# Second expert layer: GpSimd takes every second row addition of the gathered tokens

## The chip, the cores and the metric

The kernel runs on one core of one Trainium2 chip. The time is device microseconds of one execution; a comparison takes the median of several. The profile is of one execution, and its times count from the first instruction.

## The reference, cut to what matters

The program is one decoder layer. A normalised input goes through a gated delta mixer and a sparse attention mixer, then through an expert layer, and is normalised at the end. Only the second half of the expert layer matters here. There are 16384 experts, and each is one row of `expert_u` and one row of `expert_v`, both of 1024 numbers. Each of the 512 tokens picks 16 experts for each of 8 heads, so 128 in all.

```python
    def block(xb):
        ...
        eidx = jnp.take_along_axis(cidx, pos, axis=-1)
        gates = jax.nn.softmax(top_s, axis=-1)
        u = expert_u[eidx]
        vv = expert_v[eidx]
        act = jax.nn.gelu(jnp.einsum('nhkd,nd->nhk', u, xb).astype(F32), approximate=False)
        return jnp.einsum('nhk,nhkd->nd', (gates * act).astype(vv.dtype), vv)
```

The last line is the stage that is changed: for each token, the sum of its 128 rows of `expert_v`, each times its gate and its activation.

## The kernel before

The stages follow each other: input projection, delta mixer, sparse attention, output projection, routing with the first expert table (`route_stage`, to about 1453 us), the second expert table (`value_stage`, from about 1455 to 2007 us), final norm (`final_stage`). In each stage every engine has a program of its own, in the order in which it is written, and semaphores tie them together.

`value_stage` treats the tokens in two ways.

The first 384 tokens (`TD`) take the whole table. The table comes in 128 tiles `v_raw` of 128x1024. A tile's turn, number `e`, goes so:

- SyncE loads `v_raw` (L1522) and the activations `act_s` (L1525) for turn `e` four turns ahead, and once in eight turns a block of gates.
- VectorE forms `w`, activation times gate, 128x384 (L1566).
- ScalarE makes `v_hi`, the table tile rounded for the fast matmul (L1537), and `w_hi` from `w` (L1539).
- VectorE makes the remainders `v_lo` (128x1024) and `w_lo` (128x384), both at L1554.
- TensorE adds 24 matmuls to eight banks: for each of 8 slices the products high by high, high by low, low by high (L1589 to L1591). It waits for `v_low` and `w_low` of its turn. At the end it raises `second`, which frees the two buffers `v_hi` and `v_lo` of that parity. ScalarE waits for it before the `v_hi` of two turns on.

The last 128 tokens, one in each partition, take only their own rows. GpSimd gathers with an indirect DMA (L1547) row `k` of every token into one of four places of `ring`. VectorE adds it into `own`, times the column `k` of the weights `w_own` (L1574). In the trace `ring` is `va_ring`, `own` is `va_own`, `w_own` is `own_weights`. One gathered row belongs to each turn, and VectorE adds it at the end of the turn. GpSimd issues the gather of row `k` as soon as VectorE has added row `k - 4` (semaphore `added`). When all is done, TensorE transposes `own` into the banks (L1603), and the next stage adds the banks to the residual.

So VectorE's order in each turn is `w`, `v_lo`, `w_lo`, `own`. The order is written by hand.

## Time and profile before

| | us |
|---|---|
| median of 3 runs | 2022.57 |
| lowest and highest | 2022.33, 2024.21 |
| the profiled execution's own time | 2029.51 |
| its span, first to last instruction | 2027.7 |
| busy in the span: TensorE | 1777.1 |
| busy: VectorE | 1474.5 |
| busy: ScalarE | 699.0 |
| busy: GpSimd | 471.3 |

The profiled execution takes 7 us longer than the median run, of which the span leaves out 1.8 us. The three runs lie within 1.9 us of each other, 0.1%.

Busy time over the whole span mixes stages. The last quarter of the span is `value_stage` alone, and it is read by itself. A matmul's busy time is modelled, so the pace of TensorE is read from how far apart the starts of repeating operations lie, not from the mean of one. VectorE's operations overlap by some hundredths of a microsecond, so their cost in a row is also read from start to start.

### The profile page before, as it was taken

Reading aid. Unit: us, or ns where it says so; the run is one execution under the profiler, and the core shown is the slowest. Engines: PE = TensorE matmul, PEld = TensorE weight load, DVE = VectorE, ACT = ScalarE, POOL = GpSimd, SP = SyncE. Lnnn points to the kernel's source line nnn. Section 1 sums busy time; section 2 is a strip of 40 time slices with the busy share of each in tenths; the row PEclk is TensorE's granted clock in tenths of the full one; section 3 lists DMA queues with packets and bytes.
Section 4 is the critical chain, followed back from the end, with each engine's and each line's share of the span. In section 5 each row is a group of like instructions: output and inputs, shape, how many; then the busy total and the mean of one; then the engine's idle time right before and its main releaser. Section 6 shows DMA issues by size and latency. Waiting matters only on the chain. (4 is left out here: it accounts for less than half of the span.)

```text
span 2027.7 us, 29145 instructions
## 1 busy us (share of the span) xinstructions
PE 1777.1 (88%) x9881; PEld 1595.0 (79%) x9881; DVE 1474.5 (73%) x2561; ACT 699.0 (34%) x1053; POOL 471.3 (23%) x324
## 2 busy tenths in 40 slices
PE   6995789798779889669799999777599999999997
PEld 4874776434558789669699999777599999999996
DVE  4787542399532399898999999666577888887886
ACT  4652121434332233223344444222133333333333
POOL 1000000000110155444233333455422222222220
PEclk9998886758899889789899999899899999999999
DMA  3320000100213345334398888999899999999993
GB/s 107 103 81 21 1 1 0 54 0 1 73 54 102 107 140 179 92 113 142 122 327 330 320 304 335 332 329 332 286 329 355 336 362 330 363 330 361 332 363 124
DMA packets 148988, 404.23 MB, mean 199 GB/s; under 512 B 14228, under 2 KB 71700, under 8 KB 145464
## 3 DMA queue, kind: packets, MB, share of 16 engines
q1 hardware_dynamic: 108600, 243.97, 35.8%
q0 software_dynamic: 36864, 134.23, 17.8%
q10 hardware_dynamic: 3456, 25.17, 3.0%
q8 instruction: 36, 0.59, 0.1%
q14 instruction: 32, 0.26, 0.0%
HBM read 350.88 MB, written 52.44 MB: 199 GB/s over the span
## 5 line engine op out<-in xcount | busy, mean ns | idle before, releaser
L1458 PE MATMUL bank<-h_hi,rt_u_hi 128*128 128x384 f32 x1024 | 365.9, 357 | 85.4 <-POOL rt_u_lo L1267 44.0
L1589 PE MATMUL bank<-va_w_hi,va_v_hi 128*128 128x384 f32 x1024 | 343.3, 335 | 19.8 <-DVE va_w_lo L1554 19.8
L1459 PE MATMUL bank<-h_lo,rt_u_hi 128*128 128x384 f32 x1024 | 355.0, 347 | 0.0
L1460 PE MATMUL bank<-h_hi,rt_u_lo 128*128 128x384 f32 x1024 | 354.5, 346 | 0.0
L1590 PE MATMUL bank<-va_w_lo,va_v_hi 128*128 128x384 f32 x1024 | 343.2, 335 | 0.0
L1591 PE MATMUL bank<-va_w_hi,va_v_lo 128*128 128x384 f32 x1024 | 343.0, 335 | 0.0
L1221 ACT ACTIVATE rt_u_hi<-rt_u_raw 128x1024 fp32r<-128x1024 f32 x128 | 135.5, 1058 | 414.5 <-PE bank L1460 403.0
L1458 PEld LDWEIGHTS bank<-h_hi,rt_u_hi 128*128 128x128 f32 x1024 | 202.6, 198 | 94.6 <-POOL rt_u_lo L1267 42.8
L1537 ACT ACTIVATE va_v_hi<-va_v_raw 128x1024 fp32r<-128x1024 f32 x128 | 135.7, 1060 | 357.3 <-PE bank L1591 341.1
L1273 POOL DMA_INDIRECT h<-u_rows_dram,own_experts x128 | 188.6, 1474 | 285.7 <-DVE rt_waste L1367 278.2
L1554 DVE TENSOR_TENSOR va_v_lo<-va_v_raw,va_v_hi 128x1024 fp32r<-128x1024 f32 x128 | 156.8, 1225 | 103.7 <-ACT va_v_hi L1537 98.9
L1547 POOL DMA_INDIRECT va_ring<-v_dram,own_experts x128 | 129.9, 1015 | 412.3 <-DVE va_own L1574 396.5
L1589 PEld LDWEIGHTS bank<-va_w_hi,va_v_hi 128*128 128x128 f32 x1024 | 193.1, 189 | 20.0 <-DVE va_v_lo L1554 20.0
L1459 PEld LDWEIGHTS bank<-h_lo,rt_u_hi 128*128 128x128 f32 x1024 | 202.5, 198 | 0.0
L1460 PEld LDWEIGHTS bank<-h_hi,rt_u_lo 128*128 128x128 f32 x1024 | 201.8, 197 | 0.0
L1367 DVE SCALAR_TENSOR_TENSOR rt_waste<-h,rt_h_tok 128x1024 bf16<-128x1024 f32 x128 | 156.4, 1222 | 61.8 <-DMA h<-u_rows_dram,own_experts 59.0
L1590 PEld LDWEIGHTS bank<-va_w_lo,va_v_hi 128*128 128x128 f32 x1024 | 193.1, 189 | 0.0
L1591 PEld LDWEIGHTS bank<-va_w_hi,va_v_lo 128*128 128x128 f32 x1024 | 193.1, 189 | 0.0
L1267 POOL TENSOR_TENSOR rt_u_lo<-rt_u_raw,rt_u_hi 128x1024 fp32r<-128x1024 f32 x48 | 130.6, 2725 | 237.2 <-ACT rt_u_hi L1221 237.1
L1574 DVE SCALAR_TENSOR_TENSOR va_own<-va_ring,own_weights,va_own 128x1024 f32<-128x1024 f32 x128 | 163.6, 1278 | 0.0
L1360 DVE TENSOR_TENSOR rt_u_lo<-rt_u_raw,rt_u_hi 128x1024 fp32r<-128x1024 f32 x80 | 97.8, 1223 | 3.9 <-ACT rt_u_hi L1221 2.4
L878 POOL TENSOR_SCALAR_AFFINE_SELECT dsa_score<-dsa_score 128x128 f32<-128x128 f32 x3 | 0.9, 314 | 424.0 <-DVE dsa_score L911 424.0
(316 smaller groups left out, 2909.9 us busy)
## 6 DMA issues: line engine op xcount, KB each, us to landing
rt_u_raw<-u_dram SPq DMA_DIRECT2D x128, 512.0 KB
va_v_raw<-v_dram SPq DMA_DIRECT2D x128, 512.0 KB
active_scratch<-rt_act SPq DMA_DIRECT2D x128, 192.0 KB
gates_scratch<-rt_early ACTq DMA_DIRECT2D x24, 1024.0 KB
va_gate<-gates_scratch SPq DMA_DIRECT2D x16, 1536.0 KB
va_act<-active_scratch SPq DMA_DIRECT2D x128, 192.0 KB
in_raw<-w_in_dram SPq DMA_DIRECT2D x22, 512.0 KB, 3.3
query_raw<-w_query_dram SPq DMA_DIRECT2D x16, 512.0 KB, 3.3
```

The costliest lines, as they stand in the source:

```text
L1221: a(u_hi[:, j % 2, :], u_raw[:, j % 4, :], ACT.Copy).then_inc(u_high, 1)
L1273: nc.gpsimd.indirect_dma_start(out=ring[:, k % RING, :], out_offset=None, in_=u_rows, in_offset=bass.IndirectOffsetOnAxis(ap=eidx[:, k:k + ...
L1367: d.scalar_tensor_tensor(waste[:], ring[:, r, :], 1.0, h_tok[:], ALU.mult, ALU.mult, accum_out=dots[:, bass.ds(k, 1)]).then_inc(s["dot"], 1)
L1458: mm(bank, u_hi[:, j % 2, cols], hi[:, c, 0:TD], start=c == 0, stop=False)
L1459: mm(bank, u_hi[:, j % 2, cols], lo[:, c, 0:TD], start=False, stop=False)
L1460: last = mm(bank, u_lo[:, j % 2, cols], hi[:, c, 0:TD], start=False, stop=c == DC - 1)
L1537: nc.scalar.activation(v_hi[:, par, :], v_raw[:, j, :], ACT.Copy).then_inc(v_high, 1)
L1554: nc.vector.tensor_tensor(out, a, high.bitcast(F32), ALU.subtract).then_inc(done, 1)
L1574: nc.vector.scalar_tensor_tensor(own[:], ring[:, j, :], w_own[:, bass.ds(e, 1)], own[:], ALU.mult, ALU.add).then_inc(added, 1)
L1589: mm(bank, v_hi[:, j, cols], w_hi[:, j, :], start=start, stop=False)
L1590: mm(bank, v_hi[:, j, cols], w_lo[:, j, :], start=False, stop=False)
L1591: last = mm(bank, v_lo[:, j, cols], w_hi[:, j, :], start=False, stop=stop)
```

## The change

The gathered rows are split by parity. Rows with even `k` are added by VectorE as before. Rows with odd `k` are added by GpSimd, in two operations: a multiply of the row by its weight column into `term` (a `tensor_scalar`), and an addition of `term` to an accumulator of GpSimd's own, `own_odd`. GpSimd waits for its own multiply by the semaphore `weighed`, and for its own last addition by `added_odd`. It issues the gather of row `k + 4` behind row `k`: for an even row after VectorE has added it, for an odd one behind its own addition. At the end VectorE adds `own_odd` to `own` once, and TensorE waits for that. Two tiles of 4 KB a partition are new.

```diff
@@ value_stage @@
+        ring, own, own_odd, term = sb("ring", [P, RING, D]), sb("own", [P, D]), sb("own_odd", [P, D]), sb("term", [P, D])
...
             @block.gpsimd
             def _(pool):
-                for k in range(N):
-                    if k >= RING:
-                        pool.wait_ge(added, k - RING + 1)
+                def gather(k):
                     nc.gpsimd.indirect_dma_start(
                         out=ring[:, k % RING, :], out_offset=None, in_=v_rows,
                         in_offset=bass.IndirectOffsetOnAxis(ap=eidx[:, k:k + 1], axis=0)).then_inc(rows_in[k % RING], 16)
+
+                for k in range(RING):
+                    gather(k)
+                nc.gpsimd.memset(own_odd[:], 0.0).then_inc(added_odd, 1)
+                for k in range(N):
+                    if k % 2:
+                        pool.wait_ge(rows_in[k % RING], 16 * (k // RING + 1))
+                        pool.wait_ge(added_odd, k // 2 + 1)
+                        nc.gpsimd.tensor_scalar(term[:], ring[:, k % RING, :], w_own[:, k:k + 1], None,
+                                                ALU.mult).then_inc(weighed, 1)
+                        pool.wait_ge(weighed, k // 2 + 1)
+                        nc.gpsimd.tensor_tensor(own_odd[:], own_odd[:], term[:], ALU.add).then_inc(added_odd, 1)
+                    else:
+                        pool.wait_ge(added, k // 2 + 1)
+                    if k + RING < N:
+                        gather(k + RING)
...
                         minus(w_lo[:, par, :], w[:, par, :], w_hi[:, par, :], w_low)
+                        if k % 2:
+                            continue
                         dve.wait_ge(rows_in[j], 16 * turn)
                         if not (head and k == 0):
-                            dve.wait_ge(added, e)
+                            dve.wait_ge(added, 4 * u + k // 2)
                         nc.vector.scalar_tensor_tensor(own[:], ring[:, j, :], w_own[:, bass.ds(e, 1)], own[:],
                                                        ALU.mult, ALU.add).then_inc(added, 1)
...
                 run(dve, eight)
+                dve.wait_ge(added, N // 2)
+                dve.wait_ge(added_odd, N // 2 + 1)
+                nc.vector.tensor_tensor(own[:], own[:], own_odd[:], ALU.add).then_inc(added, 1)
...
-                pe.wait_ge(added, N)
+                pe.wait_ge(added, N // 2 + 1)
```

VectorE at the start of the stage before the change: the clearing of `va_own`, then the first turn and three operations of the second.

```order
L1576 MEMSET va_own 128x1024
L1566 TENSOR_TENSOR va_w<-va_act,va_gate 128x384
L1554 TENSOR_TENSOR va_v_lo<-va_v_raw,va_v_hi 128x1024
L1554 TENSOR_TENSOR va_w_lo<-va_w,va_w_hi 128x384
L1574 SCALAR_TENSOR_TENSOR va_own<-va_ring,own_weights,va_own 128x1024
L1566 TENSOR_TENSOR va_w<-va_act,va_gate 128x384
L1554 TENSOR_TENSOR va_v_lo<-va_v_raw,va_v_hi 128x1024
L1554 TENSOR_TENSOR va_w_lo<-va_w,va_w_hi 128x384
```

The same place after the change, with the first pair of turns and the first operation of the next.

```order
L1592 MEMSET va_own 128x1024
L1580 TENSOR_TENSOR va_w<-va_act,va_gate 128x384
L1568 TENSOR_TENSOR va_v_lo<-va_v_raw,va_v_hi 128x1024
L1568 TENSOR_TENSOR va_w_lo<-va_w,va_w_hi 128x384
L1590 SCALAR_TENSOR_TENSOR va_own<-va_ring,own_weights,va_own 128x1024
L1580 TENSOR_TENSOR va_w<-va_act,va_gate 128x384
L1568 TENSOR_TENSOR va_v_lo<-va_v_raw,va_v_hi 128x1024
L1568 TENSOR_TENSOR va_w_lo<-va_w,va_w_hi 128x384
L1580 TENSOR_TENSOR va_w<-va_act,va_gate 128x384
```

The operation on `va_own` stands only in every second turn, and in the others `w` of the next turn follows `w_lo` at once.

GpSimd at the start of the stage, as one piece of the difference. Before, its program there is nothing but 128 gathers.

```order
 L1143 UNCONDITIONAL_BRANCH
 L1542 UNCONDITIONAL_BRANCH
-L1547 DMA va_ring<-v_dram,own_experts 128x1024 x128
+L1545 DMA va_ring<-v_dram,own_experts 128x1024 x4
+L1551 MEMSET va_own_odd 128x1024
+L1545 DMA va_ring<-v_dram,own_experts 128x1024
+L1556 TENSOR_SCALAR va_term<-va_ring,own_weights 128x1024
+L1559 TENSOR_TENSOR va_own_odd<-va_own_odd,va_term 128x1024
+L1545 DMA va_ring<-v_dram,own_experts 128x1024 x2
+L1556 TENSOR_SCALAR va_term<-va_ring,own_weights 128x1024
```

Now the gathers stand two by two between pairs of operations: of the two, the first is that of the odd row behind GpSimd's addition, the second that of the even row, which waits for VectorE.

## Rows read from the trace of the kernel before

**Rows 1.** Three stretches: busy time (operations) by engine, granted clock, DMA share, GB/s.

```profile
1370.00:1380.00 10.00, 7.81 (x44) 7.17 (x42) 7.22 (x12) 1.63 (x3) 4.74 (x4) 1.00 0.98 341
1500.00:1600.00 100.00, 100.00 (x579) 100.00 (x578) 80.76 (x97) 35.49 (x49) 24.47 (x25) 1.00 0.96 345
1900.00:2000.00 100.00, 100.00 (x579) 100.00 (x578) 80.60 (x96) 35.49 (x49) 22.11 (x22) 1.00 0.88 312
```

**Rows 2.** Groups of 1500 to 2000 us: busy us, mean ns | idle before, and releaser.

```profile
L1589 PE MATMUL bank<-va_w_hi,va_v_hi 128*128 128x384 f32 x962 | 321.3, 334 | 0.0
...
L1554 DVE TENSOR_TENSOR va_v_lo<-va_v_raw,va_v_hi 128x1024 fp32r<-128x1024 f32 x120 | 147.0, 1225 | 96.2 <-ACT va_v_hi L1537 91.4 <-issue 4.8
L1537 ACT ACTIVATE va_v_hi<-va_v_raw 128x1024 fp32r<-128x1024 f32 x121 | 128.3, 1060 | 325.2 <-PE bank L1591 325.2
...
L1554 DVE TENSOR_TENSOR va_w_lo<-va_w,va_w_hi 128x384 fp32r<-128x384 f32 x120 | 66.2, 551 | 0.0
```

**Rows 3.** Timeline of VectorE, one turn: start us, length us, operation.

```profile
1704.75 1.23 DVE L1554 TENSOR_TENSOR va_v_lo<-va_v_raw,va_v_hi 128x1024 fp32r<-128x1024 f32 x1 [0.74 <-ACT va_v_hi L1537]
1705.89 0.55 DVE L1554 TENSOR_TENSOR va_w_lo<-va_w,va_w_hi 128x384 fp32r<-128x384 f32 x1
1706.36 1.28 DVE L1574 SCALAR_TENSOR_TENSOR va_own<-va_ring,own_weights,va_own 128x1024 f32<-128x1024 f32 x1
1707.56 0.55 DVE L1566 TENSOR_TENSOR va_w<-va_act,va_gate 128x384 f32<-128x384 f32 x1
```

**Rows 4.** Timeline at the stage's end: VectorE's last `own`, TensorE's transposes.

```profile
2001.78 1.28 DVE L1574 SCALAR_TENSOR_TENSOR va_own<-va_ring,own_weights,va_own 128x1024 f32<-128x1024 f32 x1
...
2007.14 1.04 PE L1603 MATMUL bank<-cst,va_own 128*128 128x128 f32 x8
```

**Rows 5.** Timeline of the same turn: ScalarE's `v_hi` and GpSimd's gather.

```profile
1707.88 1.06 ACT L1537 ACTIVATE va_v_hi<-va_v_raw 128x1024 fp32r<-128x1024 f32 x1 [2.75 <-PE bank L1591]
...
1707.92 1.01 POOL L1547 DMA_INDIRECT va_ring<-v_dram,own_experts  x1 [3.09 <-DVE va_own L1574]
```

**Rows 6.** Timeline, GpSimd and VectorE with two-input operations at the same time.

```profile
782.73 2.39 POOL L1267 TENSOR_TENSOR rt_u_lo<-rt_u_raw,rt_u_hi 128x1024 fp32r<-128x1024 f32 x1 [2.22 <-ACT rt_u_hi L1221]
782.96 2.44 DVE L1316 TENSOR_TENSOR rt_cand<-rt_val 128x256 f32<-128x256 f32 x1
...
967.59 2.29 DVE L1336 TENSOR_TENSOR rt_early<-rt_part_f,cst 128x2048 f32<-128x2048 f32 x1
968.11 3.97 POOL L1267 TENSOR_TENSOR rt_u_lo<-rt_u_raw,rt_u_hi 128x1024 fp32r<-128x1024 f32 x1 [10.31 <-ACT rt_u_hi L1221]
969.91 4.33 DVE L1338 TENSOR_TENSOR rt_early<-rt_early,rt_num_f 128x2048 f32<-128x2048 f32 x1
972.04 4.44 POOL L1267 TENSOR_TENSOR rt_u_lo<-rt_u_raw,rt_u_hi 128x1024 fp32r<-128x1024 f32 x1
```

**Rows 7.** GpSimd's one-input select by its line: duration ns min/median/max, shape.

```profile
L878 POOL TENSOR_SCALAR_AFFINE_SELECT dsa_score<-dsa_score x3: 294/294/353, 406.3 to 459.9; 128x128 f32<-128x128 f32 x3
...
L882 POOL TENSOR_SCALAR_AFFINE_SELECT dsa_bias<-dsa_bias x1: 1917/1917/1917, 461.5 to 461.5; 128x2048 f32<-128x2048 f32 x1
```

**Rows 8.** Timeline of `route_stage`: gathers beside VectorE's two-input operations.

```profile
1366.33 0.94 POOL L1273 DMA_INDIRECT h<-u_rows_dram,own_experts  x1 [1.27 <-DVE rt_waste L1367]
1366.44 1.22 DVE L1367 SCALAR_TENSOR_TENSOR rt_waste<-h,rt_h_tok 128x1024 bf16<-128x1024 f32 x1 [0.38 <-DMA h<-u_rows_dram,own_experts]
1367.59 1.22 DVE L1360 TENSOR_TENSOR rt_u_lo<-rt_u_raw,rt_u_hi 128x1024 fp32r<-128x1024 f32 x1
1367.95 1.68 POOL L1273 DMA_INDIRECT h<-u_rows_dram,own_experts  x1 [0.68 <-DVE rt_waste L1367]
```

5 lines of the change are left out of this document (2 added, 3 removed).

## The prediction, made before the change was run

> **What bounds the kernel now.** I read the table by stretches first. From 1500 us to the end of the second expert layer TensorE is busy all the time at a granted clock of 1.00, while VectorE is busy 81% and GpSimd 24% [rows 1]. The groups of that stretch say the same from the other side. TensorE's matmuls have 0.0 us of idle time ahead of them, and ScalarE's split of the table tile waits 325.2 us for "PE bank", which is the release of its buffer by the matmuls [rows 2]. So TensorE sets the end, and VectorE waits for ScalarE, which waits for TensorE: 91.4 us ahead of its `v_lo` [rows 2].
>
> Next the order of time within one tile, a tile being one of the 128 turns with 24 matmuls. The starts of `own` at 1706.36 and at 2001.78 lie 71 tiles apart, so a tile takes 295.42 / 71 = 4.16 us and a pair of tiles 8.32 us [rows 3, 4]. In it VectorE issues four operations. From start to start `v_lo` takes 1.14 us, `w_lo` 0.47 and `own` 1.20; `w`, of the same shape as `w_lo`, I put at 0.47. That is 3.28 us of work and 0.88 us of waiting [rows 3]. Its lead over TensorE is small: `w_lo` ends at 1706.44, and the tile before, whose end releases ScalarE's `v_hi`, ends just ahead of 1707.88 [rows 3, 5]. So `w_lo` is ready some 1.3 us before TensorE wants it. That lead, and not the 19% of idle time, is what may be spent.
>
> **What the change takes off VectorE.** One `own` in each pair: 64 times 1.20 us. TensorE does not wait for `own` in the loop, so this alone is worth nothing. VectorE's work in a pair falls from 6.56 to 5.36 us.
>
> **What it puts on GpSimd.** In each pair a multiply (one tensor input and a column) and an addition (two inputs), both 128x1024. Neither stands in this stretch now. The nearest row for the addition is GpSimd's subtraction of the same size, 2.39 us when nothing is in its way [rows 6]. For the multiply it is the one-input affine select: 0.294 us for 128 columns and 1.917 us for 2048, so 0.845 ns a column and 1.05 us for 1024 [rows 7].
>
> GpSimd by itself keeps up. A pair costs two gather issues, 1.01 us [rows 5], or 1.68 us where one meets a VectorE operation [rows 8], besides 1.05 and 2.39. That is 1.01 + 1.68 + 1.05 + 2.39 = 6.1 us of 8.32, with 2 us left for the gaps between them.
>
> **The two engines exclude each other.** This is the row on which everything turns. At 782.73 GpSimd begins its 2.39 us; VectorE's addition of two inputs, issued at 782.96, takes 2.44 us and ends 0.28 us behind GpSimd's end [rows 6]. At 967.59 VectorE begins a two-input operation of 2.29 us; GpSimd's, issued at 968.11, takes 3.97 us in place of 2.39. VectorE's next takes 4.33 and GpSimd's next 4.44: they take turns, whole instruction by whole instruction [rows 6]. All four VectorE operations of a tile read two tiles from SBUF. So the time of both engines adds up, and I take it as one queue.
>
> Prices in that queue. GpSimd's two-input operation ends 972.08 - 969.88 = 2.20 us after VectorE's end, the next 976.48 - 974.24 = 2.24 [rows 6]: 2.22 us for the addition, 0.17 less than alone, since its start is hidden. The multiply, with the same 0.17 hidden, holds the queue 0.88 us; with nothing hidden 1.05. A VectorE operation behind a GpSimd turn costs a little less than its start-to-start time: the one of 2.29 us ended 974.24 - 972.08 = 2.16 us after it, where about 2.21 would follow from the 0.08 us overlap of `v_lo` and `w_lo` [rows 3, 6]. Twice 0.05 us comes off. The sum for a pair:
>
> 5.36 + 2.22 + 0.88 - 0.10 = 8.36 us at least, 8.53 us with the multiply unhidden.
>
> Against TensorE's 8.32 us that is 0.04 to 0.21 us too much, and I take the middle, 8.44 us, since the multiply is issued right where VectorE is about to begin `w_lo` and may get ahead of it with its start unhidden. TensorE then waits for `w_lo` 0.12 us in each of 64 pairs, 7.7 us, less the 1.3 us of lead used up first: 6.4 us.
>
> The bounds. No row has a one-input GpSimd operation beside a two-input VectorE operation. If it holds nothing up, the queue has 7.48 us in a pair and TensorE stays the bound: 0 us. If the multiply costs what the two-input form does, a pair has 5.36 + 2.22 + 2.20 - 0.10 = 9.68 us: 1.36 x 64 - 1.3 = 86 us. I stay at one input, because the row with one input is near in kind and its cost is proportional to the columns [rows 7].
>
> The Trainium skill (SBUF — State Buffer, "Who interferes with whom") says that a VectorE instruction with two SBUF inputs contends with a GpSimd instruction that reads SBUF, with whoever issues first holding the shared pair for the whole instruction. The trace agrees for two inputs on both sides, as 4.33 us for an operation of 2.29 us shows. By its wording the multiply counts too, which gives the 8.36 to 8.53 us above; a rule by which only two-input GpSimd operations counted would give the 7.48 us and no loss.
>
> **The other edits.** The gathers: now each is issued 0.28 us behind the end of `own` [rows 3, 5]. The even ones stay there; the odd ones are queued behind multiply and addition, and so come 4 to 6 us later in the pair. A gather first waits for a running VectorE operation (1.68 us at 1367.95 in place of 0.94) but does not hold up the next one (1.22 us at 1366.44) [rows 8]. It is 4 rows, or 16.6 us, ahead of use, so later by 6 us it still lands in time; the DMA engines, at 96% busy and 345 GB/s [rows 1], are asked for no more bytes. Cost 0, covered by the ring. GpSimd's waiting for `added` holds up only gathers behind it, with the same cover. The `memset` of the second accumulator lies in the time before the first table tile is there: 0. VectorE's last addition of the two accumulators costs 1.2 us. It follows GpSimd's last addition, which ends 0.47 + 1.14 + 0.88 + 0.47 + 2.22 = 5.2 us behind the last `own` (`w`, `v_lo`, multiply, `w_lo`, addition), and so is over at about 6.5 us. TensorE now ends 2007.14 - 2003.06 = 4.1 us behind the `own` of the last tile [rows 4], and the last `own` will be that of the tile before, so 4.1 us further from the end, less the lead that is used up: about 7 us. Cost 0, with about 1 us of cover; without cover at most 1.2 us.
>
> TensorE's clock: 0.12 us of waiting in 8.4 should not lower it. At 1370 to 1380 us TensorE was busy 7.81 us of 10 and was still granted 1.00 [rows 1].
>
> **The forecast.** The profiled execution took 2029.51 us, the median of the runs is 2022.57 us. The change adds 6.4 us: 2035.9 us for a profiled execution, 2029.0 us for the median, 0.3% slower.
>
> **Rivals.**
> 1. No difference. The multiply does not exclude VectorE, or holds the queue less than 0.85 us. Then a pair is at most 8.38 us and the loss under 4 us: 2022.6 to 2026 us. For it: the sum misses TensorE's 8.32 us by 0.04 us at its lower end. Against it: every two-input row shows full exclusion, and what VectorE is denied is its second reader's turn, whatever GpSimd does with what it reads. This is the rival on the other side; it decides at 0.9 us of held time.
> 2. The multiply is dear, a rate above 0.845 ns a column. Each 0.1 us of it costs 6.4 us: at one and a half times the price +0.5 us, 2061 us, at the two-input price 2109 us. Against it: the one-input row. For it: that row is another operation, and it reads no scalar column.
> 3. The feed becomes the bound: odd gathers, or table tiles that are issued behind a later `v_lo`, land late at 96% DMA load [rows 1]. ScalarE never waited for a table tile in 121 turns [rows 2], and a wait of 1 us every eighth tile would be 16 us: 2045 us.
> 4. Faster. VectorE freed of `own` could only help if TensorE waited for it, and its idle time ahead of the matmuls is 0.0 us [rows 2].
>
> **How the numbers follow.** The bound of what can be told from no change is 0.2%, or 4 us. Forecast, a pair between 8.38 and 8.6 us: 50%. Rival 1: 35%. Rival 2 from 20 us upwards: 8%. Rival 3: 4%. Rival 4: 3%. Slower is the forecast and rivals 2 and 3: 0.62; same 0.35; faster 0.03. The range runs from 2021 us, which takes in rival 1 with some scatter, to 2048 us, which takes in the sum with a multiply 0.2 us dearer and rival 3; outside lie most of rival 2 and all of rival 4 that counts.
>
> **What would show it.** In the changed profile VectorE's `v_lo`, `w_lo` or `w` must show means above 1.225 and 0.551 us, by some 3 us in a pair in all, and GpSimd's addition more than 2.39 us. The multiply's shortest time should be near 1.05 us. The starts of `own` should lie 8.44 us apart, and TensorE's first matmul of a tile should have waits for `w_lo` of about 0.1 to 0.2 us. If `w_lo` and `v_lo` keep their lengths beside the multiply, rival 1 is right; if the multiply takes over 1.3 us, rival 2; if ScalarE waits for the table tile, rival 3. The forecast fails altogether if the exclusion does not add up as one queue, for example when one engine is held up without the other gaining.

## The result, and the profile after

The changed kernel takes 2107.39 us (median of 4 runs, 2105.73 to 2109.73) against 2023.39 us for the kernel before (median of 4). The ratio is 1.041, with a 95% interval of 1.039 to 1.043. So it is slower, as forecast, but by 84 us and not by 6. The time lies 59 us above the top of the forecast range. The profiled execution took 2105.73 us, its span 2103.5 us.

The first view is the groups of the changed kernel between 1500 and 2000 us. Its columns are those of [rows 2]: line, engine, operation, tiles, shapes, count, then busy time and mean ns of one, then idle time ahead and its releaser.

```profile
L1608 PE MATMUL bank<-va_w_hi,va_v_hi 128*128 128x384 f32 x832 | 282.2, 339 | 54.3 <-DVE va_w_lo L1568 54.3
...
L1556 POOL TENSOR_SCALAR va_term<-va_ring,own_weights 128x1024 f32<-128x1024 f32 x53 | 179.4, 3384 | 2.2
L1568 DVE TENSOR_TENSOR va_w_lo<-va_w,va_w_hi 128x384 fp32r<-128x384 f32 x104 | 170.9, 1643 | 0.0
L1559 POOL TENSOR_TENSOR va_own_odd<-va_own_odd,va_term 128x1024 f32<-128x1024 f32 x52 | 167.2, 3215 | 4.3
...
L1568 DVE TENSOR_TENSOR va_v_lo<-va_v_raw,va_v_hi 128x1024 fp32r<-128x1024 f32 x104 | 126.7, 1218 | 60.3 <-ACT va_v_hi L1537 60.3
```

TensorE, which had 0.0 us of idle time ahead of its matmuls [rows 2], now waits for `w_lo`. `w_lo` has grown from 551 ns to a mean of 1643, while `v_lo` kept its length. GpSimd's multiply takes 3384 ns. The waits of the same stretch (who waits for whom, us in all, times, longest) give the count:

```profile
ACT va_v_hi L1537 <- PE bank L1610: 266.3, 104, 2.8
...
PEld bank L1608 <- issue: 69.3, 52, 1.3
DVE va_v_lo L1568 <- ACT va_v_hi L1537: 60.3, 52, 1.2
PE bank L1608 <- DVE va_w_lo L1568: 54.3, 52, 1.1
POOL va_ring L1545 <- DVE va_own L1590: 30.0, 52, 0.6
```

TensorE's weight load stands still 69.3 / 52 = 1.33 us in every pair of tiles, and 64 pairs of that are 85 us. So the whole loss is TensorE standing still once in each pair. And VectorE is not the engine that is always at work: it still waits 60.3 / 52 = 1.16 us in every pair for `v_hi`, and `v_hi` waits for TensorE. Both wait, for each other.

Busy time by engine (PE, PEld, DVE, ACT, POOL), granted clock, DMA share and GB/s in a stretch of the stage, to be held against [rows 1]:

```profile
1700.00:1800.00 100.00, 89.54 (x504) 86.64 (x503) 87.81 (x74) 31.61 (x42) 91.33 (x42) 1.00 0.90 298
```

TensorE's clock stayed at 1.00, its level of 2.4 GHz, although TensorE is busy 89.5% and no more all the time. DMA fell from 345 to 298 GB/s with the pace, and nobody waits for it. GpSimd is busy 91%, and waits for `own` only 30.0 / 52 = 0.58 us in a pair.

Now one pair in order of time (start, duration, engine, operation, idle time ahead). VectorE of the changed kernel, first the `w_lo` of the pair before:

```profile
1705.50 2.74 DVE L1568 TENSOR_TENSOR va_w_lo<-va_w,va_w_hi 128x384 fp32r<-128x384 f32 x1
1708.16 1.27 DVE L1590 SCALAR_TENSOR_TENSOR va_own<-va_ring,own_weights,va_own 128x1024 f32<-128x1024 f32 x1
1709.36 0.55 DVE L1580 TENSOR_TENSOR va_w<-va_act,va_gate 128x384 f32<-128x384 f32 x1
1709.83 1.21 DVE L1568 TENSOR_TENSOR va_v_lo<-va_v_raw,va_v_hi 128x1024 fp32r<-128x1024 f32 x1
1710.96 0.55 DVE L1568 TENSOR_TENSOR va_w_lo<-va_w,va_w_hi 128x384 fp32r<-128x384 f32 x1
1711.43 1.39 DVE L1580 TENSOR_TENSOR va_w<-va_act,va_gate 128x384 f32<-128x384 f32 x1
1714.00 1.22 DVE L1568 TENSOR_TENSOR va_v_lo<-va_v_raw,va_v_hi 128x1024 fp32r<-128x1024 f32 x1 [1.19 <-ACT va_v_hi L1537]
1715.14 2.74 DVE L1568 TENSOR_TENSOR va_w_lo<-va_w,va_w_hi 128x384 fp32r<-128x384 f32 x1
1717.81 1.27 DVE L1590 SCALAR_TENSOR_TENSOR va_own<-va_ring,own_weights,va_own 128x1024 f32<-128x1024 f32 x1
```

GpSimd and ScalarE at the same time:

```profile
1709.70 1.01 POOL L1545 DMA_INDIRECT va_ring<-v_dram,own_experts  x1 [0.57 <-DVE va_own L1590]
1710.76 3.39 POOL L1556 TENSOR_SCALAR va_term<-va_ring,own_weights 128x1024 f32<-128x1024 f32 x1
1714.23 3.24 POOL L1559 TENSOR_TENSOR va_own_odd<-va_own_odd,va_term 128x1024 f32<-128x1024 f32 x1
```

```profile
1712.91 1.06 ACT L1537 ACTIVATE va_v_hi<-va_v_raw 128x1024 fp32r<-128x1024 f32 x1 [2.45 <-PE bank L1610]
```

The starts of `own` lie 1717.81 - 1708.16 = 9.65 us apart, where [rows 3, 4] give 8.32. The 9.65 us are a closed loop: a tile's turn on TensorE frees the buffers that the same side (even or odd) needs for its tile two turns on, and TensorE can't begin that tile before its `w_lo`. The even side can be walked:

- 1708.24: the `w_lo` before this pair ends (1705.50 + 2.74). TensorE begins the even tile, which takes 4.16 us.
- 1712.91: the buffer it frees lets `v_hi` start, 0.51 us after 1708.24 + 4.16. `v_hi` takes 1.06 us.
- 1714.00: `v_lo`, then `w_lo`, which would end 0.47 us behind `v_lo` but is held by the addition issued at 1714.23. The addition is held itself until `v_lo` ends at 1715.22. From there to its end at 1717.47 are 2.25 us, close to the 2.20 and 2.24 us of [rows 6].
- 1717.88: `w_lo` ends, and TensorE begins. 1717.88 - 1708.24 = 9.64 us.

Without the hold of 2.19 us (2.74 less 0.55) the loop takes 7.45 us. It has 0.87 us to spare against TensorE's 8.32, so the hold costs 2.19 - 0.87 = 1.32 us in each pair. This is no test yet, because the 0.87 us are worked out from the same pair. The kernel before gives nearly the same: there `w_lo` ends at 1706.44 and, if the same 0.51 us lie ahead of `v_hi`, the tile at 1707.88 - 0.51 = 1707.37, 0.93 us later [rows 3, 5]. Whether 0.87 us also holds for other holds and places is what the experiments show. Nothing of VectorE's 1.16 us of idle time helps, because it lies in front of the `v_lo` of this very loop. That is the theory which the experiments test: call it LOOP. The rival, QUEUE, is the prediction's own sum with a dearer multiply. A third, GPSIMD BOUND, says that GpSimd's own chain of gather, multiply, addition and gather fills the pair.

### The profile page after: what moved, and what is told of

Same layout as the page of the kernel before. It is cut to its first block and busy times, and to the rows that moved or that the text cites. A ratio compares the mean times of both kernels' runs of the same rounds, so it can differ in the third digit from the quotient of the medians.

```text
span 2103.5 us, 29156 instructions
## 1 busy us (share of the span) xinstructions
PE 1792.2 (85%) x9881; PEld 1591.9 (76%) x9881; DVE 1582.6 (75%) x2498; ACT 706.1 (34%) x1053; POOL 900.7 (43%) x453
## 5 line engine op out<-in xcount | busy, mean ns | idle before, releaser
L1608 PE MATMUL bank<-va_w_hi,va_v_hi 128*128 128x384 f32 x1024 | 348.5, 340 | 83.0 <-DVE va_w_lo L1568 83.0
L1556 POOL TENSOR_SCALAR va_term<-va_ring,own_weights 128x1024 f32<-128x1024 f32 x64 | 217.6, 3400 | 5.8 <-DVE va_own L1590 3.3
L1559 POOL TENSOR_TENSOR va_own_odd<-va_own_odd,va_term 128x1024 f32<-128x1024 f32 x64 | 202.5, 3165 | 5.3
L1568 DVE TENSOR_TENSOR va_w_lo<-va_w,va_w_hi 128x384 fp32r<-128x384 f32 x128 | 203.2, 1588 | 0.0
```

Source lines behind the costliest of these rows:

```text
L1556: nc.gpsimd.tensor_scalar(term[:], ring[:, k % RING, :], w_own[:, k:k + 1], None, ALU.mult).then_inc(weighed, 1)
L1559: nc.gpsimd.tensor_tensor(own_odd[:], own_odd[:], term[:], ALU.add).then_inc(added_odd, 1)
L1568: nc.vector.tensor_tensor(out, a, high.bitcast(F32), ALU.subtract).then_inc(done, 1)
L1608: mm(bank, v_hi[:, j, cols], w_hi[:, j, :], start=start, stop=False)
```

## The experiments

The loss or gain of each is against runs of the kernel before on the same chip; its medians there were 2022.6 to 2025.5 us. Where an edit is shown, lines with - are those of the changed kernel.

### What the GpSimd operations cost and hold

A block behind the end of the program runs each GpSimd operation alone, twice in a row, and then once beside a row of VectorE additions of two inputs, 128x1024.

```diff
+                ops = [
+                    lambda: g.tensor_scalar(term[:], row, col, None, ALU.mult),
...
+                    lambda: g.affine_select(out=term[:], in_=row, pattern=[[1, D]], base=0, channel_multiplier=1,
+                                            compare_op=ALU.is_ge, fill=0.0),
...
+                    lambda: g.tensor_tensor(term[:], row, ring[:, 1, :], ALU.add),
+                ]
```

> The changed kernel, with a block of extra operations between the second expert layer and the final norm; nothing else is changed. In the block GpSimd first works alone: each of seven operations twice (multiply by a column 128x1024, 128x512 and 128x128, multiply by a constant, the select, a copy, a two-input addition). Then VectorE issues 24 two-input additions of 128x1024 back to back beside six of GpSimd's. Three theories of the 84 us. LOOP: the multiply is long (2.8 us alone) but holds VectorE up for only 0.9 us of it; the addition then falls between v_lo and w_lo of the even tile, on the path ScalarE split, v_lo, w_lo, TensorE, which two buffers close into a loop. QUEUE: the multiply holds VectorE up for 2.2 us like a two-input operation, and the pair is the plain sum of both engines' held times. GPSIMD BOUND: GpSimd's own chain of gather, multiply, addition, gather fills the pair. Expected here: LOOP and GPSIMD BOUND: column multiply alone 2.7 to 2.9 us, about 2.6 ns a column; beside VectorE one VectorE operation grows by 0.8 to 1.1 us. QUEUE: the same operation grows by 2.2 us or more. All: addition alone 2.39 us, and one VectorE operation grows by 2.2 us beside it. The total is 30 to 70 us above the changed kernel and says nothing.

The program took 2162.49 us with the added block. GpSimd's timeline alone (x2: two in a row, the duration is of both):

```profile
2080.42 5.78 POOL L1640 TENSOR_SCALAR va_term<-va_ring,own_weights 128x1024 f32<-128x1024 f32 x2 [2.78 <-ACTq L1627]
2086.30 3.22 POOL L1641 TENSOR_SCALAR va_term<-va_ring,own_weights 128x512 f32<-128x512 f32 x2
2089.61 1.30 POOL L1642 TENSOR_SCALAR va_term<-va_ring,own_weights 128x128 f32<-128x128 f32 x2
...
2096.71 2.15 POOL L1644 TENSOR_SCALAR_AFFINE_SELECT va_term<-va_ring 128x1024 f32<-128x1024 f32 x2
```

The multiply takes 2.9 us (5.78 / 2) and the affine select of the same size 1.07. A plain copy takes 1.07 as well, a multiply by a constant 2.8. So the price in the forecast, 1.05 us, was that of the wrong operation. But what a VectorE operation of 1.21 us grows to beside the multiply, and then beside the two-input addition, is:

```profile
2108.21 2.06 DVE L1662 TENSOR_TENSOR va_v_raw<-va_v_raw 128x1024 f32<-128x1024 f32 x1
```

```profile
2118.39 3.35 DVE L1662 TENSOR_TENSOR va_v_raw<-va_v_raw 128x1024 f32<-128x1024 f32 x1
```

The multiply holds VectorE 0.85 us once, in spite of its 2.9 us. The addition holds it 2.14 us. Copy, select and both multiplies hold it alike. The held times of the forecast, 0.88 and 2.22 us, were therefore right.

### The same instructions in another order, and each half alone

First the same instructions, with each addition issued one pair later, behind the next `own`:

```diff
-                        nc.gpsimd.tensor_tensor(own_odd[:], own_odd[:], term[:], ALU.add).then_inc(added_odd, 1)
                     else:
                         pool.wait_ge(added, k // 2 + 1)
+                        if k:
+                            add(k // 2 - 1)
```

> The same instructions as the changed kernel on every engine; only GpSimd's order differs: the addition of an odd row is issued after VectorE's next own, ahead of the gather of the even row, and not right behind its multiply. LOOP: the addition now runs beside w and v_lo of the odd tile with TensorE's lead of about 1.3 us over it, and the multiply beside the even tile, so a pair falls from 9.65 us to 8.4 to 8.8 us: 2025 to 2050 us. QUEUE: the sum of held times is the same, 9.6 us a pair: 2100 to 2110 us. GPSIMD BOUND: the same work on GpSimd, so again about 9.3 to 9.7 us a pair: 2085 to 2110 us.

It took 2081.67 us (ratio 1.030, 1.026 to 1.033), 26 us less than the changed kernel. That is above the range of LOOP and just below those of QUEUE and GPSIMD BOUND, so each theory missed. GpSimd's timeline in it:

```profile
1799.19 1.60 POOL L1545 DMA_INDIRECT va_ring<-v_dram,own_experts  x1 [0.27 <-POOL va_term L1560]
1800.83 2.41 POOL L1554 TENSOR_TENSOR va_own_odd<-va_own_odd,va_term 128x1024 f32<-128x1024 f32 x1
1803.40 1.76 POOL L1545 DMA_INDIRECT va_ring<-v_dram,own_experts  x1 [0.16 <-POOL va_own_odd L1554]
1805.19 2.88 POOL L1560 TENSOR_SCALAR va_term<-va_ring,own_weights 128x1024 f32<-128x1024 f32 x1
1808.35 1.60 POOL L1545 DMA_INDIRECT va_ring<-v_dram,own_experts  x1 [0.27 <-POOL va_term L1560]
```

Here GpSimd never waits for VectorE. Its own chain is 1808.35 - 1799.19 = 9.16 us long, with gathers of 1.60 and 1.76 us that met VectorE operations, and it sets the pace. (The loop gives nearly the same here: one `v_lo` in each pair takes 2.95 us, held 1.74, and 8.32 + 1.74 - 0.87 = 9.19 us. That GpSimd waits for nobody is what speaks for its chain.) The chain is a second bound, which the forecast had put at 6.1 us and gaps. GPSIMD BOUND is right for this kernel in its mechanism, though not in its range.

Then the multiply without the addition (the odd rows are missing from the sum), and the addition without the multiply (the odd rows are added without their weights):

```diff
                                                 ALU.mult).then_inc(weighed, 1)
                         pool.wait_ge(weighed, k // 2 + 1)
-                        nc.gpsimd.tensor_tensor(own_odd[:], own_odd[:], term[:], ALU.add).then_inc(added_odd, 1)
```

> The changed kernel without GpSimd's additions: the weighed odd rows are left out of the sum, so the output lacks them. LOOP: the multiply holds 0.9 us once a pair, inside TensorE's lead: 8.32 us a pair, 2023 us, as before the change. QUEUE: 5.26 + 2.2 = 7.5 us of held time, below TensorE's 8.32: also 2023 us. GPSIMD BOUND: 2023 us. What it tells: that it is the addition, where it stands, and not the multiply by itself, that costs; over 2030 us would speak against LOOP.

2031.25 us, ratio 1.004 (1.002 to 1.006). `v_lo` of 2.10 to 2.22 us shows the hold of 0.9 to 1.0 us, most of which the 0.87 us to spare takes up. It still costs 8 us. The expectation had said that over 2030 us would speak against LOOP, so this run does, by 1 us, and the rest of the 8 us is not explained.

```diff
-                        nc.gpsimd.tensor_scalar(term[:], ring[:, k % RING, :], w_own[:, k:k + 1], None,
-                                                ALU.mult).then_inc(weighed, 1)
-                        pool.wait_ge(weighed, k // 2 + 1)
-                        nc.gpsimd.tensor_tensor(own_odd[:], own_odd[:], term[:], ALU.add).then_inc(added_odd, 1)
+                        nc.gpsimd.tensor_tensor(own_odd[:], own_odd[:], ring[:, k % RING, :], ALU.add).then_inc(added_odd, 1)
```

> The changed kernel without GpSimd's multiplies: the odd rows are added without their weights. LOOP: the addition comes 3.4 us earlier in the pair, between v_lo and w_lo of the odd tile, which has 1.3 us of lead for 2.2 us of hold at first; the wait moves own back, and the phases settle at 0 to 0.3 us a pair: 2023 to 2042 us. QUEUE: 5.26 + 2.22 = 7.5 us: 2023 us. GPSIMD BOUND: 2023 us. Above 2060 us would mean that the addition costs wherever it stands.

2066.57 us, ratio 1.022 (1.019 to 1.025), above what any of the theories said. In this kernel GpSimd is idle 3.2 to 4.2 us in a pair, and VectorE has 5.36 + 2.2 = 7.6 us of work. Neither is full; 44 us are lost all the same. A sum of held times cannot give this. The loop can, if every pair is read and not one. VectorE's `v_lo` of the side beside the addition is held in turns by 2.09 and 1.14 us (over its 1.21), and the starts of `own` lie 9.5 and 8.5 us apart in turns, all through 1500 to 2000 us:

```profile
1809.43 3.30 DVE L1566 TENSOR_TENSOR va_v_lo<-va_v_raw,va_v_hi 128x1024 fp32r<-128x1024 f32 x1 [1.01 <-ACT va_v_hi L1537]
...
1818.93 2.35 DVE L1566 TENSOR_TENSOR va_v_lo<-va_v_raw,va_v_hi 128x1024 fp32r<-128x1024 f32 x1 [1.98 <-ACT va_v_hi L1537]
```

Less 0.87 us each, that is 1.22 and 0.27 us in two pairs, 32 times: 48 us, near the 44.

The same addition alone, but issued right behind `own`, ahead of both gathers:

```diff
+                for k in range(0, N, 2):
+                    pool.wait_ge(added, k // 2 + 1)
...
+                    nc.gpsimd.tensor_tensor(own_odd[:], own_odd[:], ring[:, (k + 1) % RING, :], ALU.add).then_inc(added_odd, 1)
                     if k + RING < N:
                         gather(k + RING)
+                        pool.wait_ge(added_odd, k // 2 + 2)
+                        gather(k + 1 + RING)
```

> As the run with the addition only (odd rows added without their weights, 2067 us), but GpSimd issues the addition at once behind VectorE's own, before the two gathers and not between them, some 1.0 us earlier. Same instructions on each engine. LOOP: the addition then runs beside w of the odd tile and the 0.9 us in which VectorE waits anyway, so it delays v_lo by only 1.4 us, against a lead of about 1.3: 8.32 to 8.5 us a pair, 2023 to 2035 us. A theory in which each two-input turn of GpSimd costs the same wherever it is: 2067 us.

2040.08 us, ratio 1.008 (1.006 to 1.010), 5 us above the range of LOOP. The instructions are those of the run before, and moving the addition by one gather is worth 27 us. Here too the holds take turns:

```profile
1804.58 2.55 DVE L1565 TENSOR_TENSOR va_v_lo<-va_v_raw,va_v_hi 128x1024 fp32r<-128x1024 f32 x1 [0.80 <-ACT va_v_hi L1537]
...
1813.33 2.04 DVE L1565 TENSOR_TENSOR va_v_lo<-va_v_raw,va_v_hi 128x1024 fp32r<-128x1024 f32 x1 [1.29 <-ACT va_v_hi L1537]
```

One is of 1.34 us, 0.47 more than the slack, the other of 0.83 us and inside it: 0.47 x 32 = 15 us, and 15 were measured.

### The forecast's own prices: the short operation first

If only the length of the multiply was wrong, a kernel with an operation of 1.05 us in its place, which copies the odd row and leaves out its weight, should land on the forecast.

```diff
-                        nc.gpsimd.tensor_scalar(term[:], ring[:, k % RING, :], w_own[:, k:k + 1], None,
-                                                ALU.mult).then_inc(weighed, 1)
+                        nc.gpsimd.affine_select(out=term[:], in_=ring[:, k % RING, :], pattern=[[1, D]], base=0,
+                                                channel_multiplier=1, compare_op=ALU.is_ge,
+                                                fill=0.0).then_inc(weighed, 1)
```

> The changed kernel with the select in place of the multiply: it copies the row, without the weight, so odd rows are added unweighted; it holds VectorE for the same 0.84 us but is over in 1.07 us in place of 2.88. This is the price that the prediction took. LOOP: the addition is issued about 1.8 us earlier than in the changed kernel, behind the odd tile's v_lo, which has some lead; as with the addition alone (8.8 us a pair) part of it is spent: 8.5 to 9.0 us, 2035 to 2068 us. If the prediction's sum was right but for the multiply's length: 8.44 us, 2029 us. If only held time counted: same as the changed kernel, 2107 us.

2112.6 us, ratio 1.047 (1.040 to 1.055): with the forecast's own prices the loss is 88 us. This is the run that condemns the sum. Its timelines, GpSimd and then VectorE:

```profile
1804.46 2.40 POOL L1560 TENSOR_TENSOR va_own_odd<-va_own_odd,va_term 128x1024 f32<-128x1024 f32 x1
```

```profile
1804.53 3.42 DVE L1569 TENSOR_TENSOR va_v_lo<-va_v_raw,va_v_hi 128x1024 fp32r<-128x1024 f32 x1 [2.03 <-ACT va_v_hi L1537]
...
1814.18 3.42 DVE L1569 TENSOR_TENSOR va_v_lo<-va_v_raw,va_v_hi 128x1024 fp32r<-128x1024 f32 x1 [2.03 <-ACT va_v_hi L1537]
```

The addition is issued 0.07 us ahead of `v_lo` and holds it 2.21 us. By the slack that is (2.21 - 0.87) x 64 = 86 us. A pair takes 9.65 us again, as in the changed kernel, since the hold lies in the same loop, one operation earlier. VectorE is idle 2.03 us and GpSimd 3.18 us in the pair. The expectation of LOOP, 2035 to 2068 us, was missed too: the theory had the mechanism but placed the addition wrongly. The place repeats itself because the addition is issued behind `own`, and `own` moves with the loop.

### The loop opened: four buffers

If the two buffers close the loop, four places each for `v_hi`, `v_lo`, `w`, `w_hi` and `w_lo` open it.

```diff
-        v_hi, v_lo = sb("v_hi", [P, 2, D], F32R), sb("v_lo", [P, 2, D], F32R)
+        v_hi, v_lo = sb("v_hi", [P, 4, D], F32R), sb("v_lo", [P, 4, D], F32R)
...
-                        if not (head and k < 2):
-                            act.wait_ge(second, e - 1)
+                        if not (head and k < 4):
+                            act.wait_ge(second, e - 3)
```

> The changed kernel with four places instead of two for v_hi, v_lo, w, w_hi and w_lo, so that VectorE and ScalarE may be up to three tiles ahead of TensorE; the work and GpSimd's order are the same. LOOP: the loop TensorE, split, v_lo, addition, w_lo, TensorE no longer closes over one tile, so the pair falls from 9.65 us to the larger of the held times (5.26 + 2.2 + 0.84 = 8.3 us) and GpSimd's own chain (1.0 + 2.9 + 2.4 + 1.0 to 1.8 and gaps, 7.7 us and what it waits for VectorE): 8.4 to 9.2 us, 2028 to 2080 us. GPSIMD BOUND: GpSimd is as loaded as before, so the time stays at 2090 to 2107 us. QUEUE is already ruled out by the late addition (2082 us with the same held times).

2062.28 us, ratio 1.018 (1.017 to 1.020): 45 us of the 84 are gone, with all of the change's instructions there. What is left has another cause. GpSimd's additions in it:

```profile
1798.51 3.13 POOL L1559 TENSOR_TENSOR va_own_odd<-va_own_odd,va_term 128x1024 f32<-128x1024 f32 x1
...
1807.46 3.12 POOL L1559 TENSOR_TENSOR va_own_odd<-va_own_odd,va_term 128x1024 f32<-128x1024 f32 x1
```

They lie 8.95 us apart, and between them GpSimd waits for nobody (busy 93.6%, the rest are gaps between its own instructions). VectorE is nearly as full, 97%, because `own` is held here as well, 1.4 us. But it does wait for GpSimd, for rows that are gathered late, 12.0 us in all and 10 times between 1500 and 2000 us, while GpSimd never waits for VectorE. So GpSimd's chain with the long multiply is taken as the bound: (8.95 - 8.32) x 64 = 40 us, and 38 were measured. How much of the chain is VectorE's doing, which holds GpSimd's addition 0.7 us, this run does not separate.

Now the four buffers with the short operation, in which both GpSimd's chain and the loop are out of the way:

```diff
-        v_hi, v_lo = sb("v_hi", [P, 2, D], F32R), sb("v_lo", [P, 2, D], F32R)
+        v_hi, v_lo = sb("v_hi", [P, 4, D], F32R), sb("v_lo", [P, 4, D], F32R)
...
-                        nc.gpsimd.tensor_scalar(term[:], ring[:, k % RING, :], w_own[:, k:k + 1], None,
-                                                ALU.mult).then_inc(weighed, 1)
+                        nc.gpsimd.affine_select(out=term[:], in_=ring[:, k % RING, :], pattern=[[1, D]], base=0,
+                                                channel_multiplier=1, compare_op=ALU.is_ge,
+                                                fill=0.0).then_inc(weighed, 1)
```

> Four places for v_hi, v_lo and the rest, and the select in place of the multiply (odd rows without weights). With two places this first operation gave 2113 us. GpSimd's chain is now short (1.05 + 2.4 and two gathers), and VectorE is decoupled from TensorE, so the prediction's sum should hold: 5.36 + 2.2 + 0.84 - 0.1 = 8.3 us against TensorE's 8.32: 2023 to 2032 us. If the exclusion cost something beyond the sum: 2050 us or more.

2030.33 us, ratio 1.003 (1.000 to 1.005). VectorE's timeline:

```profile
1804.00 1.27 DVE L1591 SCALAR_TENSOR_TENSOR va_own<-va_ring,own_weights,va_own 128x1024 f32<-128x1024 f32 x1
...
1806.80 1.39 DVE L1569 TENSOR_TENSOR va_w_lo<-va_w,va_w_hi 128x384 fp32r<-128x384 f32 x1
1808.12 2.74 DVE L1581 TENSOR_TENSOR va_w<-va_act,va_gate 128x384 f32<-128x384 f32 x1
...
1812.39 1.27 DVE L1591 SCALAR_TENSOR_TENSOR va_own<-va_ring,own_weights,va_own 128x1024 f32<-128x1024 f32 x1
```

A pair takes 8.39 us, with VectorE never idle, one hold of 0.84 and one of 2.19 us. That is the forecast's sum of 8.36 to 8.53 us. The loss of 7 us (1 to 10 by the interval) goes with the forecast's 6.4, but is too small to tell more. The same work in two buffers takes 2112.6. So the sum was right for a kernel whose loop is open, and this kernel's is not.

The control, the kernel before with four buffers (its diff is against the kernel before):

```diff
-        act_s, w = sb("act", [P, 4, TD]), sb("w", [P, 2, TD])
-        w_hi, w_lo = sb("w_hi", [P, 2, TD], F32R), sb("w_lo", [P, 2, TD], F32R)
+        act_s, w = sb("act", [P, 4, TD]), sb("w", [P, 4, TD])
+        w_hi, w_lo = sb("w_hi", [P, 4, TD], F32R), sb("w_lo", [P, 4, TD], F32R)
```

> The control: the kernel before with four places in place of two. TensorE is the bound, so nothing changes: 2021 to 2027 us.

2026.24 us, ratio 1.002 (1.000 to 1.003). More buffers give nothing by themselves; the 3 us more are hardly clear of the noise, and leave 4 us between this kernel and the one ahead of it.

Together the runs make a table of two by two, in us above the kernel before:

| | multiply, 2.9 us | select, 1.07 us |
|---|---|---|
| two buffers | 84 | 88 |
| four buffers | 38 | 7 |

Either the closed loop or GpSimd's long chain is enough to break the forecast. Both have to go before it holds.

### The same time on GpSimd without its reads

In place of multiply and addition, GpSimd writes `term` with memsets, and the odd rows are missing from the sum. Six of them first:

```diff
+                def fill(n):
+                    for _ in range(n):
+                        nc.gpsimd.memset(term[:], 0.0).then_inc(weighed, 1)
...
-                        nc.gpsimd.tensor_scalar(term[:], ring[:, k % RING, :], w_own[:, k:k + 1], None,
-                                                ALU.mult).then_inc(weighed, 1)
-                        pool.wait_ge(weighed, k // 2 + 1)
-                        nc.gpsimd.tensor_tensor(own_odd[:], own_odd[:], term[:], ALU.add).then_inc(added_odd, 1)
+                        fill(6)
```

> The changed kernel with six clearings of a 128x1024 tile (0.96 us each, writes alone) in the place of the multiply and the addition; the odd rows are left out of the sum. GpSimd is as busy as in the changed kernel (some 5.8 us and two gathers in a pair), and its chain behind own is as long. LOOP: what costs is the hold on VectorE's two-input operations between the split and w_lo; if a write alone does not hold them, 2023 to 2027 us. GPSIMD BOUND (its occupancy or its late gathers cost): 2060 us and more. If writes hold VectorE too, v_lo and w_lo will be long in the trace.

2064.02 us, ratio 1.020 (1.016 to 1.023). No VectorE operation was held (`v_lo` 1.225 us), yet the time rose: six memsets take 6.04 us and make with waits and gathers too long a chain, so that rows came late. VectorE's `own` waited 62.2 us in all for them, 23 times. So a chain that is too long costs without any hold, which is what GPSIMD BOUND had said. Five memsets, 5.03 us, are near the 2.88 + 2.39 us of the two operations alone, and fit into the pair:

```diff
-                        fill(6)
+                        fill(5)
```

> The changed kernel with five clearings (5.0 us) in the place of multiply and addition, which take 2.88 + 2.39 = 5.27 us when nothing is in their way; the odd rows are left out of the sum. Six clearings gave 2064 us, with GpSimd never waiting and rows landing late. LOOP: writes hold nothing and five fit: GpSimd's chain is about 0.3 + 1.0 + 5.0 + 0.3 + 1.0 = 7.6 us of 8.32, so 2023 to 2030 us. GPSIMD BOUND: 2050 us and more.

2022.16 us, ratio 1.000 (0.997 to 1.002). Its groups between 1500 and 2000 us:

```profile
L1556 POOL MEMSET va_term<- 128x1024 f32 x300 | 287.7, 959 | 16.4 <-issue 2.6
...
L1572 DVE TENSOR_TENSOR va_v_lo<-va_v_raw,va_v_hi 128x1024 fp32r<-128x1024 f32 x119 | 145.8, 1225 | 165.2 <-ACT va_v_hi L1537 165.2
```

GpSimd works as long in a pair as the two operations do alone, its gathers stand where the change puts them, `own` is halved: no loss, and `v_lo` keeps its 1225 ns. So 5 us of GpSimd's time and the later gathers cost nothing. What memsets lack is a read of SBUF beside VectorE, and copy, select, multiply and addition, which read, all hold it. The run shows also that taking `own` off VectorE gains nothing.

The Trainium skill (SBUF — State Buffer, "Who interferes with whom") says that VectorE with two SBUF inputs contends with GpSimd instructions that read SBUF and not with those that only write. This run agrees, with 1225 ns.

### One addition at four places

The addition alone (again without the weights), with one or two memsets ahead of it that hold nobody, so that it comes 1 or 2 us later:

```diff
+                        fill(2)
+                        nc.gpsimd.tensor_tensor(own_odd[:], own_odd[:], ring[:, k % RING, :], ALU.add).then_inc(added_odd, 1)
```

> The run with the addition only (2067 us), with two clearings (1.9 us) ahead of each addition, so that it is issued some 3.4 us behind own and not 1.3. More work for GpSimd, the odd rows without weights. LOOP: in a pair at TensorE's pace w_lo of the odd tile is over 3.0 us behind own and v_lo of the even tile starts at 5.4; the addition's hold of 2.2 us falls into that hole: 8.32 us a pair, 2023 to 2028 us, so the kernel gets 40 us faster by added work. If only held time or GpSimd's load counted: 2067 us or more.

2037.96 us, ratio 1.005 (1.003 to 1.007): 29 us less than without the memsets, though GpSimd has 2 us more work in a pair. The expectation, 2023 to 2028, was still too low. With one memset:

```diff
-                        fill(2)
+                        fill(1)
```

> The addition only, with one clearing ahead of it, so that it is issued about 2.3 us behind own; without a clearing 2067 us, with two 2038 us (odd rows without weights). LOOP: at 2.3 us it catches w_lo of the odd tile: 2045 to 2075 us, no faster than without. A theory in which more distance is simply better: 2050 us, halfway.

2101.8 us, ratio 1.039 (1.036 to 1.042), slower than both its neighbours, and beyond what was expected. In GpSimd's and VectorE's timelines of it, the addition is issued 0.14 us ahead of `v_lo`:

```profile
1806.56 2.40 POOL L1565 TENSOR_TENSOR va_own_odd<-va_own_odd,va_ring 128x1024 f32<-128x1024 f32 x1
```

```profile
1806.70 3.35 DVE L1575 TENSOR_TENSOR va_v_lo<-va_v_raw,va_v_hi 128x1024 fp32r<-128x1024 f32 x1 [2.00 <-ACT va_v_hi L1537]
```

With two memsets it is issued 1.14 us ahead of it:

```profile
1806.68 2.41 POOL L1565 TENSOR_TENSOR va_own_odd<-va_own_odd,va_ring 128x1024 f32<-128x1024 f32 x1
```

```profile
1807.82 2.35 DVE L1575 TENSOR_TENSOR va_v_lo<-va_v_raw,va_v_hi 128x1024 fp32r<-128x1024 f32 x1 [1.94 <-ACT va_v_hi L1537]
```

The four places, by how long behind the end of `own` the addition is issued:

| addition issued | kernel | median us | above its kernel before | by hold less 0.87 us |
|---|---|---|---|---|
| at once | alone, ahead of the gathers | 2040.1 | 15 | 15 |
| after one gather, 1.3 us | alone | 2066.6 | 44 | 48 |
| 2.3 us | one memset ahead | 2101.8 | 78 | 81 |
| 3.3 us | two memsets ahead | 2038.0 | 13 | 17 |

What counts is how much of the addition is left when `v_lo` begins. At one memset `v_lo` is held 3.35 - 1.21 = 2.14 us: less 0.87 to spare, 1.27 x 64 = 81 us, and 78 were measured. At two it is held 1.14 us: 0.27 x 64 = 17 us, and 13 were measured. One instruction, at places 1 us apart, costs 13 or 78 us. The slack of 0.87 us, taken from the changed kernel, gives the cost of these four kernels within 5 us; these sums take the held times from the runs themselves, while the expected ranges, for which the phases were guessed, were missed.

### Two ways out that did not work

ScalarE multiplies the odd rows (an activation with the weight column as scale), and GpSimd only adds them, right behind `own`:

```diff
+                        if k % 2:
+                            act.wait_ge(rows_in[j], 16 * (2 * u + k // 4 + 1))
...
+                            nc.scalar.activation(term[:, (k // 2) % 2, :], ring[:, j, :], ACT.Copy,
+                                                 scale=w_own[:, bass.ds(e, 1)]).then_inc(weighed, 1)
```

> A complete version: ScalarE multiplies the odd row by its weight (a scaled copy behind its w_hi, 1.06 us, no share in the contention seen so far), and GpSimd only adds, at once behind VectorE's next own. Expected by LOOP: as the run before it, 2023 to 2035 us, so the offload costs next to nothing but gains nothing either, since TensorE is the bound. If ScalarE's longer turn delays its split of the even tile: 2040 us or more.

2041.61 us, ratio 1.007 (1.004 to 1.010), 7 us above the range of LOOP. Its `v_lo` is held as in the run that added at once (2.52 and 2.08 us long in turns), which accounts for most of the 17 us. It computes everything and saves 66 us of the 84, but is not faster than the kernel before. Then with a gather and two memsets ahead of the addition, the place that had been good for it:

```diff
+                def add(n):
+                    fill(2)
+                    pool.wait_ge(weighed, n + 1)
...
                     if k + RING < N:
                         gather(k + RING)
+                    if k:
+                        add(k // 2 - 1)
```

> A complete version: ScalarE multiplies the odd rows (as in the run of 2042 us), and GpSimd issues the gather of the even row, two clearings and then the addition, so that the addition falls into the same hole. LOOP: 2023 to 2030 us. It can't be faster than the kernel before, since TensorE stays the bound; about 2042 us would mean that the 15 us of that run came from ScalarE's longer turn and not from the addition's place.

2090.66 us, ratio 1.032 (1.029 to 1.035): failed, by a mechanism that no theory had named. (The expectation was 2023 to 2030 us.) A wait of it between 1500 and 2000 us:

```profile
ACT va_term L1545 <- DMA va_ring<-v_dram,own_experts: 109.3, 36, 5.9
```

The odd row's gather is issued later, lands late, and ScalarE blocks on it with `v_hi` queued behind: 3 us each of 36 times. ScalarE is on the path, and a wait put into its program costs.

Last, the changed kernel with both gathers behind the addition:

```diff
                     nc.gpsimd.tensor_tensor(own_odd[:], own_odd[:], term[:], ALU.add).then_inc(added_odd, 1)
                     if k + RING < N:
                         gather(k + RING)
+                        gather(k + 1 + RING)
```

> A complete version with the very instructions of the changed kernel on every engine; only the gather of the even row moves behind the addition. Multiply and addition then start 1.0 us sooner behind own. LOOP: the multiply is over 3.4 to 3.6 us behind own, the addition holds VectorE to about 5.9 us, half a microsecond into v_lo of the even tile, inside the lead; what is left is GpSimd's chain, 2.9 + 2.4 + two gathers of 0.94 to 1.76 and gaps, 8.0 to 9.0 us: 2023 to 2062 us. If the sum of the work alone counted: 2107 us as the changed kernel.

2100.86 us, ratio 1.036 (1.032 to 1.039), outside of what was expected. `w_lo` is held as in the changed kernel (mean 1643 ns), and GpSimd waits for nobody either, so its chain, multiply 3.40 and addition 3.21 us with their waits, and the loop both take about 9.6 us. Moving gathers does not free the addition from `v_lo`.

## Why the prediction was wrong, step by step

**What bounds the kernel before**: right. TensorE is the bound, and the writes-only run shows that VectorE's relief is worth nothing.

**The engines exclude each other, and the held times**: right. 2.22 us were predicted for the addition; `w_lo` grew by 2.19. 0.88 were predicted for the multiply; `w` grew by 0.84.

**The multiply's duration**: wrong, and with it "GpSimd by itself keeps up". 1.05 us was taken from the affine select [rows 7]; its shortest in the changed kernel is 2.87. This was rival 2's condition, but not its price: it was to cost by holding VectorE 2.20 us, and it holds 0.84. Rival 2's 2109 us is near the measured 2107.39 by chance. The length does matter for GpSimd's chain: predicted at 6.1 us and gaps, it takes 8.95 us with four buffers. Of the difference 1.8 us are the multiply, 0.7 us the addition, which VectorE holds, and the rest gaps. With the loop open this costs 38 us.

**"I take it as one queue"**: this is the step that failed, also at the forecast's own prices (88 us with the select). The sum of 8.44 us a pair assumes that whoever is held has other work or a buffer to fall back on, so that only the total counts. With four buffers and a short operation it does, and a pair takes 8.39 us. With two, the loop (tile, `v_hi`, `v_lo`, `w_lo`, tile) is closed, and a hold in it costs all of its length beyond the slack. The prediction had the number: "That lead, and not the 19% of idle time, is what may be spent." But it then spent it once, 1.3 us for the whole stage, where the hold needs it anew in every pair. From its own rows it could have had (2.22 - 1.3) x 64 = 59 us, 2081 us, with the addition so that all of its hold falls on one `v_lo` or `w_lo`. The rest to 84 us is the size of the lead: 1.3 us was measured from the end of `w_lo` to the release of `v_hi`, and the loop has 0.87, since 0.51 us lie between the end of `w_lo` plus a tile and the next `v_hi`.

**Where the addition falls**: looked at only for the multiply ("right where VectorE is about to begin `w_lo`"). The place decides between 13 and 78 us for the same addition.

**Rival 1**, no difference: its reason, a multiply that holds less than 0.85 us, is just met, and did not matter.

**Feed, clock, memset**: right for the changed kernel. No wait for a gather or a table tile stands in its waits. The clock stayed at 1.00.

**The end of the stage**: slightly off. The last addition of the two accumulators was to be hidden with 1 us of cover. In VectorE's timeline of the changed kernel it waits for GpSimd:

```profile
2081.65 1.22 DVE L1597 TENSOR_TENSOR va_own<-va_own,va_own_odd 128x1024 f32<-128x1024 f32 x1 [3.91 <-POOL va_own_odd L1559]
```

TensorE's transposes wait 0.56 us for it, within the bound of 1.2.

**What would show it**: the held time was to be some 3 us in a pair, and is 2.19 + 0.84. But `own` is 9.65 us apart and not 8.44, with TensorE waiting 1.1 to 1.3 us and not 0.1 to 0.2. The last sentence of the prediction named the true failure, the exclusion that does not add up as one queue, and gave it no chance and no price.

**What stays open.** The multiply alone costs 8 us. Its `v_lo` is held in turns by about 1.0 and 0.9 us, which less 0.87 us each accounts for 2 to 8, and for 5 if they are averaged. In the four-buffer kernel `own` grows by 1.4 us beside a multiply that is issued 0.46 us behind it, and not by 0.84. And where an addition is going to fall follows from the phases into which both engines settle; the experiments measure these, and no expectation had them right. None of this was taken apart.

No version beat the kernel before. The best that offloads the rows completely takes 2041.61 us.

## What to carry to other kernels

Before adding up the times that two engines take from each other, find the loop that the buffers close, and its slack in each turn; a hold inside it costs its length less that slack, each time round, however idle both engines look. Then look where the moved instruction is issued against the operations of that loop, since one microsecond decides. And price a GpSimd operation by a row of the same operation: its length (for GpSimd's own chain) and the time it holds VectorE are two numbers.

## What the runs showed of the hardware

- GpSimd's multiply by a column takes 0.65, 1.6 and 2.9 us for 128, 512 and 1024 columns, 2.5 ns a column, and by a constant 2.8 us; copy and affine select take 1.07 us for 1024. The Trainium skill (GPSIMD Engine Reference, "Engine selection") calls one-input operations roughly line-rate. Copy and select agree, if VectorE's 1.21 us for its two-input addition of that size is the measure, with 1.07 us; the multiply, at 2.9, does not.
- All of these one-input operations hold a two-input VectorE operation the same 0.84 us, the two-input addition holds it 2.14 to 2.2 us, a memset not at all. The Trainium skill (SBUF — State Buffer, "Who interferes with whom") says that the pair is locked for the whole instruction; for the multiply the measurement says less than a third of it.
- Beside the multiply, one VectorE operation passed unheld before the next was held: at 1710.96 `w_lo` took 0.55 us, and `w` at 1711.43 took 1.39, with the multiply issued at 1710.76.
- A gather's issue grew from 1.01 to 1.60 and 1.76 us where it was issued while VectorE had `own` or `v_lo` under way, as in [rows 8].
- GpSimd's addition, 2.38 us alone, took 3.24 us when it was issued 0.23 us behind a `v_lo` of 1.22 us.
